# Neighbourhood attention: eight banks a step apart, division moved to GpSimd, output made transposed

## The reference

```python
def neighbourhood_attention(q, k, v, rpb):      # T = 1024 tokens = 16 rows of 64, 8 heads of 64
    row_start = jnp.clip(rows - KH // 2, 0, R - KH)          # KH = 8 rows of keys
    scores = jnp.einsum('bhrqd,bhrikd->bhrqik', qg, k_rows).astype(jnp.float32)
    scores = scores * (dh ** -0.5)
    ...
    scores = jnp.where(in_win[None, None, None, :, None, :], scores + bias[None], -jnp.inf)
    p = jax.nn.softmax(scores.reshape(B, H, R, W, KH * W), axis=-1).reshape(B, H, R, W, KH, W)
    out = jnp.einsum('bhrqik,bhrikd->bhrqd', p.astype(v.dtype), v_rows)

def hybrid_mixer(h, ln_g, w_in, rpb, gu_f, gb_f, gu_b, gb_b, norm_g, w_out):
    proj = n @ w_in
    qa, ka, va, qg, kg, vg, rg, zf, zb = jnp.split(proj, offsets, axis=-1)
    y_na = neighbourhood_attention(na_heads(qa), na_heads(ka), na_heads(va), rpb)
    y_gla = bidirectional_gla(qg, kg, vg, rg, zf, zb, gu_f, gb_f, gu_b, gb_b, norm_g)
    return jnp.concatenate([y_na, y_gla], axis=-1) @ w_out
```

## Time and profile before

| | |
|---|---|
| three runs, median (lowest to highest) | 3662.8 us (3661.44 to 3667.34) |
| the profiled execution: its time / its span | 3664.23 us / 3661.8 us |
| PE busy over the span | 3344.4 us (91%) |
| DVE, ACT, POOL busy | 962.3, 645.5, 402.3 us |
| mean granted clock of TensorE | 0.955 of full speed |
| GLA with filler, first GLA matmul to last filler | 2139.8 to 2372.7 us |
| GLA without filler | 2372.7 to 2419.08 us |
| neighbourhood attention | 2419.08 to 2653.02 us |

### The profile page before, as it was taken

One profiled execution on the slowest core, in us unless ns is written; L12 is line 12 of the kernel. 1 busy time (PEld: TensorE's weight loads), 2 busy tenths in 40 slices (PEclk: granted clock), 3 DMA queues, 4 the chain that ended last, 5 costly groups with the idle time before them and its releaser, 6 DMA issues. The chain is left out here.

```text
span 3661.8 us, 30554 instructions
## 1 busy us (share of the span) xinstructions
PE 3344.4 (91%) x12062; PEld 1950.8 (53%) x12062; DVE 962.3 (26%) x1880; ACT 645.5 (18%) x1469; POOL 402.3 (11%) x479
## 2 busy tenths in 40 slices
PE   4997898888949999999959999977799999999999
PEld 2444444887427777777734455455544444444444
DVE  4224344564131111111123133455511000000101
ACT  3000222222211111111112121135521000000000
POOL 2003242542220000000012000100000000000000
PEclk9998999999969999999979999978899999999999
DMA  5434732002129988898843100120021111132222
GB/s 211 132 87 65 219 35 45 1 24 81 69 99 413 367 333 328 337 337 335 338 163 115 52 0 12 28 74 1 3 90 46 40 36 40 40 122 79 95 77 75
DMA packets 248554, 461.71 MB, mean 126 GB/s; under 512 B 27952, under 2 KB 110288, under 8 KB 244944
## 3 DMA queue, kind: packets, MB, share of 16 engines
q1 hardware_dynamic: 224433, 398.39, 32.4%
q0 software_dynamic: 9360, 34.08, 2.5%
q10 hardware_dynamic: 14608, 27.14, 1.9%
HBM read 481.33 MB, written 61.97 MB: 148 GB/s over the span
## 5 line engine op out<-in xcount | busy, mean ns | idle before, releaser
L1767 PE MATMUL bank<-e_w,e_xsT 128*128 128x256 f32 x2240 | 491.5, 380 | 1.6 <-DVE e_xsT L1807 1.6
L1767 PEld LDWEIGHTS bank<-e_w,e_xsT 128*128 128x128 f32 x2240 | 427.1, 191 | 74.9 <-issue 18.2
L2840 PE MATMUL bank<-w_ff,uT 128*128 128x512 f32 x1024 | 440.2, 592 | 3.6 <-DVE hT L2897 3.6
L2809 PE MATMUL bank<-hT,w_ff 128*128 128x512 f32 x1024 | 439.8, 592 | 0.0
L2840 PEld LDWEIGHTS bank<-w_ff,uT 128*128 128x128 f32 x1024 | 194.4, 190 | 249.2 <-issue 243.1
L2809 PEld LDWEIGHTS bank<-hT,w_ff 128*128 128x128 f32 x1024 | 194.4, 190 | 243.9 <-issue 243.9
L1786 PE MATMUL bank<-e_w,e_hidT 128*128 128x512 f32 x560 | 246.1, 592 | 0.0
L473 PE MATMUL bank<-w_in,hT 128*128 128x512 f32 x512 | 224.2, 599 | 4.0 <-DVE hT L385 2.3
L2112 PE MATMUL bank<-w_gla,nT 128*128 128x512 f32 x384 | 168.6, 599 | 1.3 <-ACT nT L2076 1.3
L758 PE MATMUL bank<-hT,w_qkv 128*128 128x512 f32 x384 | 167.0, 593 | 0.0
L1786 PEld LDWEIGHTS bank<-e_w,e_hidT 128*128 128x128 f32 x560 | 103.7, 190 | 117.2 <-issue 117.2
(11 more groups left out here) (453 smaller groups left out, 3847.6 us busy)
## 6 DMA issues: line engine op xcount, KB each, us to landing
e_w<-in_w SPq DMA_DIRECT2D x144, 2048.0 KB
w_ff<-in_w_ff SPq DMA_DIRECT2D x96, 512.0 KB, 3.6
wa<-in_w_ada SPq DMA_DIRECT2D x24, 1024.0 KB, 6.4
y_rows<-e_y ACTq DMA_DIRECT2D x35, 512.0 KB, 7.0
y_rows<-zero SPq DMA_DIRECT2D x1, 16384.0 KB, 113.7
w_in<-in_w_in SPq DMA_DIRECT2D x4, 2048.0 KB, 15.7
w_qkv<-in_w_in SPq DMA_DIRECT2D x12, 512.0 KB, 6.8
w_gla<-in_w_in SPq DMA_DIRECT2D x3, 2048.0 KB, 14.8
```

The costliest lines, as they stand in the source:

```text
L1767: t = pe.matmul(experts_up_bank(k, part, j), b.xsT[n][:, f, :], w[:, f, part * HALF:(part + 1) * HALF], start=f == 0, stop=f == NK - 1)
L2809: t = pe.matmul(k.bank[2 * (j % 2) + h][:, :], w[:, f, :], hT[:, f, h * BANK:(h + 1) * BANK], start=f == 0, stop=f == NK - 1)
L2840: t = pe.matmul(k.bank[2 * n + h][:, :], b.uT[:, f, m * P:(m + 1) * P], b.ring[j % SLOTS][:, h * BANK:(h + 1) * BANK], start=f == 0, stop= ...
```

## The change

1. The loop over rounds is gone. Each bank has one stream through all of its eight units (`near_rows`), with eight steps for a unit, and bank n begins n steps later (`pause(n)`). In the steady state every step holds, on each engine, one bank's turn of every kind.
2. The output product has its operands exchanged, so that it comes out transposed: the turn (L2616) and ScalarE's dividing copy ahead of it (L2559) are gone. ScalarE copies the diagonal blocks straight to `n_qkT`.
3. The division moves ahead of the transposes: GpSimd multiplies `n_sc` (128x512) by the inverted sums in place (new L2600).
4. `tensor_reduce` negates the maximum itself; the instruction that did it (L2580) is gone.
5. The rate of the filler in GLA goes from 2.2 to 1.8 matmuls a round (`NEAR_RATE`).

```diff
+NEAR_RATE = 1.8
-    weave(rounds(*(gla_tensor(k, s[n], b[n], mix_b.qkvr, decay_b.la, n) for n in two)), fill, 2.2)
+    weave(rounds(*(gla_tensor(k, s[n], b[n], mix_b.qkvr, decay_b.la, n) for n in two)), fill, NEAR_RATE)
...
-    for r in range(ROWS // 2):
-        interleave(*(near_scalar(k, s, b, r, n) for n in range(NSETS)))
...
+    interleave(*(near_scalar(k, s, b, n) for n in range(NSETS)))
+    interleave(*(near_vector(k, s, b, n) for n in range(NSETS)))
+    interleave(*(near_gpsimd(k, s, b, n) for n in range(NSETS)))
+    interleave(*(near_tensor(k, s, b, n) for n in range(NSETS)))
...
-    a.activation(b.ob[n], k.bank[n][:, 0:P], ACT.Copy, scale=b.st[n][:, 3:4]).then_inc(*s.ob_ready.up().inc)
...
+        v.tensor_reduce(st[:, 0:1], sc[:, :], AX.X, ALU.max, negate=True).then_inc(*s.neg_max.up().inc)
...
+    for u, _, _ in near_rows(n):
+        yield from pause(4)
+        g.wait_ge(*s.exp_ready(u + 1))
+        g.wait_ge(*s.sum_inverse(u + 1))
+        g.tensor_scalar(b.sc[n][:, :], b.sc[n][:, :], b.st[n][:, 2:3], None, ALU.mult).then_inc(*s.weights_ready.up().inc)
+        yield from pause(4)
...
+    pe, bank = k.nc.tensor, k.bank[n]
+    yield from pause(n)
+    for u, i, p in near_rows(n):
...
+        yield
+        pe.wait_ge(*s.q_ready(u + 1))
+        if u >= NSETS:
+            pe.wait_ge(*s.mix_out(u - NSETS + 1))
+        pe.matmul(bank[:, :], b.q2[n][:, :], b.qkT[:, PAIRS + p, lo * W:(lo + KH) * W], start=True, stop=True).then_inc(*s.scored.up().inc)
+        yield from pause(4)
+        pe.wait_ge(*s.weights_ready(u + 1))
+        pe.wait_ge(*s.neg_max(u + 1))
+        transposes(k, bank, b.sc[n]).then_inc(*s.rows_turned.up().inc)
+        yield from pause(2)
+        pe.wait_ge(*s.pT_out(u + 1))
+        for q in range(4):
+            t = pe.matmul(bank[:, 0:P], val[:, lo // 2 + q, p * P:(p + 1) * P], b.pT[n][:, q * P:(q + 1) * P], start=q == 0, stop=q == 3)
+        t.then_inc(*s.av_made.up().inc)
+        yield
```

More of the change, by code:

```diff
@@ L2225, in gla @@
         next(fill)
-    weave(rounds(*(gla_scalar(k, s[n], b[n], mix_b.qkvr, decay_b.ng, n) for n in two)), fill, 2.2)
+    weave(rounds(*(gla_scalar(k, s[n], b[n], mix_b.qkvr, decay_b.ng, n) for n in two)), fill, NEAR_RATE)
     interleave(*(gla_vector(k, s[n], s[1 - n], b[n], mix_b.qkvr, oacc, n) for n in two))
@@ L2567, in near_vector @@
[L2567 to L2589, removed]
-        yield
@@ L2593, in near_tensor, with near_scalar @@
[L2593 to L2612, removed]
-    yield
-    yield
-    pe.wait_ge(*s.ob_ready(u + 1))
-    pe.transpose(bank[:, 0:P], b.ob[n], k.c("ident")).then_inc(*s.o_turned.up().inc)
-    yield
+def near_scalar(k, s, b, n):
+    a, q2, sc, st = k.nc.scalar, b.q2[n], b.sc[n], b.st[n]
+    yield from pause(n)
+    for u, i, p in near_rows(n):
+        at = slice(i * W, (i + 1) * W)
+        if u >= NSETS:
+            a.wait_ge(*s.scored(u - NSETS + 1))
+        a.activation(q2[0:W, 0:W], b.qkT[0:W, p, at], ACT.Copy, scale=NAD ** -0.5).then_inc(*k.A.up().inc)
+        a.activation(q2[W:P, W:P], b.qkT[W:P, p, at], ACT.Copy, scale=NAD ** -0.5).then_inc(*s.q_ready.up().inc)
+        yield from pause(3)
+        a.wait_ge(*s.neg_max(u + 1))
+        a.activation(sc[:, :], sc[:, :], ACT.Exp, bias=st[:, 0:1], accum_out=st[:, 1:2]).then_inc(*s.exp_ready.up().inc)
+        yield from pause(5)
+        a.wait_ge(*s.av_made(u + 1))
+        a.activation(b.qkT[0:W, p, at], k.bank[n][0:W, 0:W], ACT.Copy).then_inc(*k.A.up().inc)
+        a.activation(b.qkT[W:P, p, at], k.bank[n][W:P, W:P], ACT.Copy).then_inc(*s.mix_out.up().inc)
@@ new lines, in near_vector @@
+def near_vector(k, s, b, n):
+    v, V, sc, st = k.nc.vector, k.V, b.sc[n], b.st[n]
+    yield from pause(n)
+    for u, i, p in near_rows(n):
+        _, dr = near_window(i)
+        yield from pause(2)
+        v.wait_ge(*s.scored(u + 1))
+        if u >= NSETS:
+            v.wait_ge(*s.rows_turned(u - NSETS + 1))
+        m = V.up()
+        v.tensor_tensor(sc[:, :], k.bank[n][:, :], b.bias[:, p, dr * W:(dr + KH) * W], ALU.add).then_inc(*m.inc)
+        v.wait_ge(*m)
+        v.tensor_reduce(st[:, 0:1], sc[:, :], AX.X, ALU.max, negate=True).then_inc(*s.neg_max.up().inc)
+        yield from pause(2)
+        v.wait_ge(*s.exp_ready(u + 1))
+        v.reciprocal(st[:, 2:3], st[:, 1:2]).then_inc(*s.sum_inverse.up().inc)
+        yield from pause(2)
+        v.wait_ge(*s.rows_turned(u + 1))
+        if u >= NSETS:
+            v.wait_ge(*s.av_made(u - NSETS + 1))
+        v.tensor_copy(b.pT[n][:, :], k.bank[n][:, :]).then_inc(*s.pT_out.up().inc)
+        yield from pause(2)
```

40 lines of the change are left out of this document (15 added, 25 removed).

## The result

The changed kernel took **3553.66 us** (median of 4 runs, 3553.21 to 3556.73) against 3662.38 us of the kernel before in the same session; the ratio is 0.9697, 95% interval 0.9683 to 0.9711.

A forecast was written before the change was run, and what follows sets the result against it. Engines waiting for each other in turn, none full, were taken to bound the attention. 3664.2 - 79 (attention) - 10 (GLA) = 3575, median 1.4 lower: 3574 us; own range 3560 to 3588, wider range 3558 to 3602.

The forecast's parts named there:

- the step of the attention: Neighbourhood attention: one unit per step of 2.35 us, 2.25 of PE work plus 0.10 for waits.
- the waits in GLA with its filler: GLA: PE's existing 5.5 us of waits grow by 4, plus 1 us in the second part.
- PE sets the step: Attention: PE's turn of 2.25 us exceeds DVE's 2.10 and ACT's 1.85, so PE sets the pace.
- the sum of 2.25: Attention, PE's work per unit at full clock: scores 0.87, transposes 0.49, product 0.89 us.
- The rest of the formula: Attention: about 11 us start, 58 full steps, about 8 us end; 155 us in all at step 2.35.
- The slack of the ring: Attention: PE, DVE and ACT need each other's previous-step results; some tenths of a us to spare, so PE sets the step.
- the first rival: Attention: hand-overs cost more than 0.1 us and no engine is full; step 2.8, section 181, 3600 us; chance 0.18.
- The tail of GLA: Between last filler and attention: SyncE's late loads of val_odd and biases take 17 us, no longer covered by GLA.
- near bounds: POOL's multiplication per unit: 0.43 us from memset, 1.42 from half a two-input operation; far bound 2.84, taken as 0.9.
- POOL beside DVE: Attention: by the port rule DVE and POOL do not block each other; otherwise each of 64 steps carries POOL's time.
- rival 3: Attention: small gaps keep TensorE at half clock; step 4.4, section 276, 3695 us, slower than before; chance 0.03.
- Rival 4: Attention: a wait still orders whole rounds, so no overlap; at most 23.5 us gained, 3629 us with GLA; chance 0.03.

The follow-up runs named there:

- The kernel with the later waits: Changed kernel with the bias issued before the odd values; DVE and PE wait for them only at first use, not before the stage: 3545.91 us.
- the negation apart: Changed kernel with the negation of the maximum again a separate DVE instruction behind a wait: 3560.08 us, section 153.7 us.
- Without the stagger: Changed kernel without pause(n), so all eight banks are in the same step: 3682.02 us, ratio 1.0044 to the kernel before.
- the kernel with the later waits and the rate 1.6: Changed kernel with bias issued first, bias and odd values awaited only at first use, and filler rate 1.6 for 1.8: 3547.54 us.

## Why the prediction came out 20 us too slow

The profiled execution was forecast at 3575 us and took 3554.1: -21.1, of which 7.1 in the attention, 9.8 in GLA and 4.2 ahead of both. The mechanism was right; the steps that failed are two terms of the sum that were mis-sized, both by waits that did not come: the step of the attention, 2.35 us for a measured 2.21, and the waits in GLA with its filler, 10.5 us for 2.5.

- **PE sets the step: right.** Work added to PE, POOL and DVE, one at a time, gives 173.5, 209.8 and 166.4 us of section, each by the load of the fullest engine; the negation's 153.7 us do not follow that rule. PE never left the chain, the clock was 1.00, the scores never ran in a row of 16, and the time behind the attention stayed.
- **The size of the step: wrong by 0.14.** "I add 0.10 for waits that are nearly on time: 2.35" is the first failed step: 0.02 came (2.21 less 2.19 of PE's work). The other 0.06 is the sum of 2.25, mostly the transposes: 20 in 2.43 us contain the pipeline of the last one, and their distance is 0.11, not 0.12. The rest of the formula stands: 11 + 58 x 2.214 + 8 = 147.4, and the trace has 10.7, 128.4 and 8.8, together 147.9.
- **The slack of the ring: smaller than the forecast's "some tenths".** An instruction of 0.15 us on DVE uses it up, and each step grows by (18.33 - 17.71) / 8 = 0.08 us. The forecast counted the negation as 0.06 us of DVE's load and 0.15 on the way to exp and gave it no share of the gain; put back, it costs 6 us. This is the first rival's mechanism at a far smaller price than its step of 2.8. VectorE's order ahead of the prediction is to be read so: addition and maximum serve the same bank (n_sc 13510 and n_st 13526 are both bank 5), and only copy and inverse serve others, so the maximum, and the negation behind it, follow the addition directly.
- **GLA's waits: wrong, and the largest term.** "I let them grow by 4" and "plus 1 for waits" put 10.5 us of waiting into GLA, the 5.5 of the earlier trace rows among them. PE waited 2.5 us from GLA's first product to the last filler. This is the second failed step, worth 8.0 us. What is left is PE's own work: by the terms of the forecast 202.4 + 36 + 3.5 = 242 us, measured 240.1. With the waits the stretch is 242.7 us, forecast 252.7 (the forecast's rounding to -10 takes 0.4 of this back). PE's waits for DVE's `oacc` were 2.55, 1.69 and 0.42 us before and are one of 1.28 and three of 0.42 now; the kernel before with 1.8 has the same four, so it is the rate that changes them. How it does so stays open. The forecast's bounds were no added waits and longer ones; that they could shrink was not considered.
- **The tail of GLA: right.** The DMAs are late next. From the last filler's end to the attention 16.8 us passed, forecast 17; SP's waits are 7.4 and 5.3 us. The kernel with the later waits takes them off the path and gets back what GLA's own end leaves, about 8 us.
- **POOL: 1.56 us, outside of both near bounds** (0.43 and 1.42) and inside the far one (2.84). It did no harm, as "up to about 2.0 us POOL costs nothing" says; the transposes waited 1.5 us for it in all, at the start and the end of the stage. With the negation apart the same 1.56 us did cost something, so the 2.0 hold only for the ring as changed. The nearest row was no guide: one tensor to read is not cheaper than two.
- **POOL beside DVE: no contention that matters.** DVE's rows of 128x512 are 684 to 690 ns with POOL busy for 69% and for 97%; with POOL idle, in the kernel before, they were 684, 686 and, for the copy, 671. By the Trainium skill (SBUF — State Buffer, section Who interferes with whom) a DVE instruction contends with GpSimd only if it has two SBUF inputs or runs in a two-port mode. This trace agrees; no run puts such an instruction beside POOL in this stage.
- **The clock: rival 3 did not come.** 1.00 in every steady window. With the negation apart PE idles 0.6 us a round and stays at 1.00; with 18% idle, in the kernel that doubles POOL's work, it is 0.91. The Trainium skill (TensorE: Matmul & The Clock Gate, section A second HAM failure mode: psum-queue depth-cycling) tells of a kernel whose frequent short idles between groups of matmuls make the clock oscillate; the idles of 0.6 us a round here did not.
- **Rival 4 was not the case.** Without the stagger the whole change, the new rate with it, would have been a loss of 16 us.

The 4.2 us ahead of GLA are not explained. Kernels with the same program there spread over 5 us. Without them the time would have been 3557.9, at the low end of the range: that it fell 4 us outside is in part chance, the two terms are not.

## What to carry to other kernels

Where engines hand work round in a ring and none is full, set the units one step apart before moving work between engines; moved work is hidden only behind units that are elsewhere in the ring, and in lockstep it lengthens the chain. Forecast the step as the largest load with next to no surcharge (here 0.02 us over PE's work, 0.07 over POOL's), then test the ring's slack with the smallest instruction, since a negation can cost more than its length. When filler is spread out, sum the work of the engine that it fills: if that sum exceeds what the others need, it is the time, and the next thing late is what waited behind the filler.

## What the runs showed of the hardware

- A multiplication of 128x512 f32 by a column of 128x1 takes 1563 ns on POOL, 1488 ns by a constant, and 486 ns on DVE. An operation of POOL with two 128x512 inputs took 1271 ns, so the form with fewer inputs was the slower.
- The transfer of the bias and the odd values, 3.9 MB, moved at 245 GB/s over the 16 us ahead of the attention. In the kernel with the later waits and the rate 1.6 the bias held DVE back until 2392.7, 9.6 us behind its issue at 2383.1, with two w_out halves of 2 MB each issued from 2385.3 on. Whether they slowed it is not shown: at 1.8, with w_out issued 7 us behind the bias, DVE's first addition came 10.0 us behind it and waited only for the scores.
